# A three-block transformer kernel on one Trainium2 core: products of ones on an idle TensorE, and expert weights loaded expert by expert

## The reference

```
def moe(h, w_router, b_router, w_gate, b_gate, w_up, b_up, w_down, b_down):
    logits = jnp.dot(h, w_router) + b_router
    top_logit, top_idx = lax.top_k(logits, TOP_K)          # 4 of 32
    gates = jax.nn.softmax(top_logit, axis=-1)
    ...
    def expert_block(args):                                # rows of one expert
        xb, e = args
        g = jnp.minimum(xb @ w_gate[e] + b_gate[e], SWIGLU_LIMIT)
        u = jnp.clip(xb @ w_up[e] + b_up[e], -SWIGLU_LIMIT, SWIGLU_LIMIT)
        act = g * jax.nn.sigmoid(SWIGLU_ALPHA * g) * (u + 1)
        return act @ w_down[e] + b_down[e]
    ...
```

## Time and profile before

| | us |
|---|---|
| median of 3 runs | 2707.42 |
| lowest, highest | 2702.99, 2712.85 |
| profiled execution | 2703.1 |
| its span in the trace | 2701.4 |
| TensorE busy | 2512.8 (93%) |
| VectorE, ScalarE busy | 1056.0, 370.9 |
| read from memory | 726.30 MB |
| the half products of the experts, L1498: gate and up, down | 475.9, 240.4 |

### The profile page before, as it was taken

The page is one execution under the profiler, slowest core; times in us unless marked ns, Lnnn a source line. Parts: engine busy times, 40 slices in busy tenths (PEclk is TensorE's granted clock), DMA queues, the critical chain, the costliest instruction groups (busy, mean ns, idle before and its releaser), DMA issues. The chain is left out here.

```text
span 2701.4 us, 33603 instructions
## 1 busy us (share of the span) xinstructions
PE 2512.8 (93%) x12943; PEld 1534.0 (57%) x12944; DVE 1056.0 (39%) x2206; ACT 370.9 (14%) x747; POOL 43.0 (2%) x64
## 2 busy tenths in 40 slices
PE   6998999999999799997999989998999999988998
PEld 2543333333333233335878857867876887756786
DVE  1243122221121122224382258756996433244433
ACT  2122111111111111111122110011002000132001
POOL 0000000000000000000000000000100000000000
PEclk8998999999999899998989999999999999999999
DMA  8604999999997899998433368844997543141442
GB/s 333 264 9 165 427 429 429 428 429 428 428 429 335 341 428 429 428 410 313 167 125 133 148 222 331 289 162 155 379 380 273 195 166 109 69 156 36 144 165 100
DMA packets 188020, 728.26 MB, mean 270 GB/s; under 512 B 9758, under 2 KB 103292, under 8 KB 159156
## 3 DMA queue, kind: packets, MB, share of 16 engines
q1 hardware_dynamic: 168324, 651.29, 61.6%
q0 software_dynamic: 19632, 76.09, 7.1%
HBM read 726.30 MB, written 1.05 MB: 269 GB/s over the span
## 5 line engine op out<-in xcount | busy, mean ns | idle before, releaser
L1498 PE MATMUL bank<-experts_raw,experts_xs 128*64 128x512 f32 x2112 | 475.9, 600 | 15.9 <-DMA experts_raw<-in_w_up 13.6
L1498 PEld LDWEIGHTS bank<-experts_raw,experts_xs 128*64 128x64 f32 x2112 | 147.9, 138 | 334.5 <-issue 295.1
L2384 PE MATMUL bank<-big,ffn_actT 128*128 128x512 f32 x704 | 309.1, 592 | 0.0
L1498 PE MATMUL bank<-experts_raw,tiled_act_s 128*64 128x512 f32 x1056 | 240.4, 601 | 51.7 <-DMA experts_raw<-in_w_down 50.5
L1797 PE MATMUL bank<-hT,ring 128*128 128x256 f32 x1024 | 225.0, 383 | 4.1 <-DMA ring<-in_w_in 2.9
L1797 PEld LDWEIGHTS bank<-hT,ring 128*128 128x128 f32 x1024 | 196.7, 192 | 32.9 <-issue 5.8
L2384 PEld LDWEIGHTS bank<-big,ffn_actT 128*128 128x128 f32 x704 | 130.6, 190 | 148.3 <-issue 148.3
L1632 DVE COPY tiled_spread<-bank 128x256 f32<-128x256 f32 x33 | 14.0, 425 | 441.2 <-PE bank L1534 441.2
L1498 PEld LDWEIGHTS bank<-experts_raw,tiled_act_s 128*64 128x64 f32 x1056 | 71.1, 137 | 199.1 <-issue 122.4
L2259 PEld LDWEIGHTS bank<-hT,big 128*128 128x128 f32 x1408 | 164.4, 193 | 18.5 <-issue 18.5
L2259 PE MATMUL bank<-hT,big 128*128 128x128 f32 x1408 | 165.5, 276 | 0.3 <-DVE hT L454 0.3
(11 more groups left out here) (478 smaller groups left out, 2629.3 us busy)
## 6 DMA issues: line engine op xcount, KB each, us to landing
experts_raw<-in_w_gate SPq DMA_DIRECT2D x64, 2048.0 KB, 23.7
experts_raw<-in_w_up SPq DMA_DIRECT2D x64, 2048.0 KB, 25.1
experts_raw<-in_w_down SPq DMA_DIRECT2D x64, 2048.0 KB, 25.5
big<-in_ffn_w_gu SPq DMA_DIRECT2D x88, 1024.0 KB, 9.4
ring<-in_mod_w POOLq DMA_DIRECT2D x30, 2048.0 KB, 10.7
big<-in_ffn_w_down SPq DMA_DIRECT2D x44, 1024.0 KB, 5.0
ring<-in_w_in SPq DMA_DIRECT2D x16, 2048.0 KB, 8.6
mla_wm<-in_w_mod SPq DMA_DIRECT2D x24, 1024.0 KB, 6.7
```

Source lines behind the costliest of these rows:

```text
L1498: last = nc.tensor.matmul(bank[b][h * HALF:(h + 1) * HALF, :], stationary(kt), raw[p][:, k, h * C:(h + 1) * C], start=kt == 0, stop=kt == ...
L2384: last = nc.tensor.matmul(bank[b][:], actT[:, s, f, t * P:(t + 1) * P], wd[:, s, f, n * 512:(n + 1) * 512], start=start and f == 0, stop=s ...
```

## The change

It has two parts. A new helper, `warm(pe, b, n)`, lets TensorE compute n products of a 128 x 128 matrix of ones with itself into bank b; nobody reads them. It stands at 14 places in the program's text, at ends of stages, at the start of the norms that have their sum of squares already (`squared`), and at a few places inside the second block, the pooling mixer and the differential attention. In the numbers of one run it makes 9, 19, 5, 6 and 32 products in the first block, 6, 10 and 26 in the second, and 116 in the third: 229. The experts' stage gets another order: SP loads gate, up and down of one expert behind one another, and TensorE computes down of item e-1 right behind gate of item e.

```diff
+    def warm(self, pe, b, n):
+
+        for _ in range(n):
+            self.nc.tensor.matmul(self.bank[b][:, 0:P], self.ones[:], self.ones[:], start=True, stop=True)
...
@@ Norm.tensor
         for b in range(4):
             core.claim(pe, b)
+        if self.squared:
+            core.warm(pe, 0, 5)
         for t in range(TT):
...
@@ end of mla_norm, of mla_heads, of route
+                core.copied(pe, 7)
+                core.warm(pe, 7, 9)
...
+                core.warm(pe, 1, 19)
...
+            core.copied(pe, 5)
+            core.warm(pe, 5, 6)
...
@@ experts_tiled, SP
-            load(1, 0)
-            load(1, 1)
-            with sp.Fori(2, E) as e:
-                load(e, 0)
-                load(e, 1)
-                load(e - 1, 2)
-            load(E - 1, 2)
+
+            with sp.Fori(1, E) as e:
+                for m in range(3):
+                    load(e, m)
             core.first_w_in_2(sp)
...
@@ experts_tiled, TensorE
             with pe.Fori(1, items) as e:
-                gate_up(e)
+
+                expert = gate(e)
+                down(e - 1)
+                gather(e + 1)
                 turn(e + 1, g_rows, g_copied, G, g_turned)
+                up(e, expert)
                 spreading(e - 1, x_copied, e + 1)
-                down(e - 1)
                 after(pe, spread_ready, e)
                 turn(e + 1, x_rows, x_copied, X, x_turned)
                 turn(e + 1, u_rows, u_copied, U, u_turned)
                 scatter(e - 1)
...
             scatter(n - 1, True)
+            core.warm(pe, Y, 32)
...
@@ experts_tiled, ScalarE
             with act.Fori(1, items) as e:
-                take_gu(e)
+                take_g(e)
                 take_y(e - 1)
+                take_u(e)
                 take_x(e + 1)
...
@@ second
+                if h < 2:
+                    core.warm(pe, 0, (6, 10)[h])
                 core.claim(pe, b)
...
+            core.copied(pe, 7)
+            core.warm(pe, 7, 26)
...
@@ ffn, end; pool_mixer, start and end
+            core.copied(pe, 7)
+            core.warm(pe, 7, 9)
...
+            core.claim(pe, 4)
+            core.warm(pe, 4, 7)
             pe.wait_ge(*norm.normed.next(pe, TT))
...
+            core.warm(pe, 4, 9)
...
@@ diff_attention
+                core.claim(pe, b)
+                if h == H3 - 2:
+                    core.warm(pe, b, 6)
                 pe.wait_ge(*S["prob_ready"].next(pe, TT))
-                core.claim(pe, b)
...
+            core.copied(pe, 4)
+            core.warm(pe, 4, 10)
...
+                core.claim(pe, q)
+                if q == 0:
+                    core.warm(pe, q, 14)
                 pe.wait_ge(*S["o_ready"].next(pe))
-                core.claim(pe, q)
...
+            core.copied(pe, 7)
+            core.warm(pe, 7, 9)
```

More of the change, by code:

```diff
@@ L1500, in product, with gate @@
                     last.then_inc(used[p], 1)
-            def gate_up(e):
+            def gate(e):
                 after(pe, xs_ready, e)
@@ L1506, in gate_up, with up @@
                 product(expert, 0, G, lambda kt: tiles(xs)[:, kt % 4, kt // 4, :])
-                gather(e + 1)
+                return expert
+            def up(e, expert):
                 after(pe, u_taken, e)
@@ L1547, in scatter @@
                             op.then_inc(*core.filled[2 * t + h].up())
-            gate_up(0)
+            first = gate(0)
+            gather(1)
+            up(0, first)
             turn(1, g_rows, g_copied, G, g_turned)
@@ L1588, in take_y, with take_g, take_u @@
                 run(ys[:], bank[Y][:], ACT.Copy).then_inc(y_copied, 1)
-            def take_gu(e):
+            def take_g(e):
                 after(act, used[PARTS - 1], e + 1)
                 run(g_rows[:], bank[G][:], ACT.Copy).then_inc(g_copied, 1)
+            def take_u(e):
                 take_rows(e + 1)
@@ L1597, in take_gu @@
                 run(sig[:], gate[:], ACT.Sigmoid, scale=SWISH).then_inc(sig_ready, 1)
-            take_gu(0)
+            take_g(0)
+            take_u(0)
             take_x(1)
             with act.Fori(1, items) as e:
-                take_gu(e)
+                take_g(e)
                 take_y(e - 1)
+                take_u(e)
                 take_x(e + 1)
```

## The result

The changed kernel takes 2716.95 us (median of 6 runs, 2710.65 to 2722.73), the kernel before 2706.82 beside it. The ratio is 1.0041, 95% interval [1.0021, 1.0061]: 0.4% slower. 2719 was forecast, with +11.6 against the median of before; +10.1 came. The profiled execution of after is the shortest of the six (2710.65, span 2709.0).

The account below looks back on a forecast made before the run. Weight transfers were taken to bound the experts. To the profiled 2703.1 us it added 29.4 for the order and −18 for the ones, giving 2714.5; the median, 4.3 above, was forecast at 2719, range 2693 to 2744.

Parts of the forecast that it names:

- Bound: Experts: weight transfers at 428 GB/s set the pace, 29.36 us a round; TensorE's own round is shorter, 26.59.
- The steady round: Experts' loop: down's buffer comes free late, the queue runs dry 0.85 us a round, over 27 rounds +23.0.
- Start: Loop's first gate at clock 0.52 makes down's buffers late: +3.4 us.
- Expert with two items: Expert 20: the 15.07 us wait for down goes, gate, up and down of expert 21 wait instead: −4.0 us.
- Tail: Experts' end: last gate and up behind one more pair of transfers, +9.8 us; shorter work from that gate, −2.8.
- The ones: 229 products of ones keep TensorE's clock full: −21 and −1.5 gain, +4.5 cost, net −18 us.
- eleven stretches: Low-clock stretches at starts of stages, holding 51.66 us of TensorE work at half speed; full clock would save 25.8.
- The costs of the ones: Ends of stages: products of 0.28 us each running past the other engines' work, 4.5 us in total.
- Rival 1: Experts: the queue never runs dry, the 23.0 us vanish, total 2696; chance 0.22.
- rival 2: Ones do not hold or restore the clock where it matters, or run at low clock themselves; total 2740, chance 0.15.
- Rival 3: Clock falls in the experts' rounds, down's buffers come free later: +46 us, total 2765; chance 0.1.

Follow-up runs that it names:

- e3: Changed kernel with TensorE computing down of item e-1 ahead of gate of item e, ones kept; 2692.73 us, 0.9955 of the kernel before.
- e5: e3 plus VectorE's gate part ahead of the spread tokens' copy and turn u ahead of turn x; 2685.07 us, 0.9908 of the kernel before.
- e4: Changed kernel with the next item's gather ahead of down of item e-1 instead of behind it; 2768.14 us, 1.0225 of the kernel before.
- e2: Changed kernel without any products of ones, only the new experts' order; 2733.02 us, 1.0097 of the kernel before.
- e8: Changed kernel with 44 products of ones instead of 32 behind the experts' last scatter; 2715.83 us, 1.0038 of the kernel before.
- e1: Kernel before with its old experts' order, plus all 229 products of ones; 2696.79 us, 0.9959 of the kernel before.
- e7: The order of e5 without any products of ones; 2696.73 us, 0.9965 of the kernel before.
- e6: Kernel before plus only the ones ahead of the experts (9, 19, 5 and 6 products); 2707.05 us, 1.0016 of the kernel before.

## Why the prediction was right, step by step

- **Bound.** The transfers of weights set the pace, and TensorE's longer work in a round did not matter. Right: e3 to e5 move the time by moving when a buffer comes free.
- **The steady round (+23.0 forecast).** Mechanism right: down's buffer comes free 12.0 after gate's landing (12.2 forecast), the load lands 8.1 later (8.2), the queue runs dry. e3 takes the dry time away, e4 enlarges it by what was forecast. The size was off: 0.63 a round instead of 0.85, so 27 x 0.63 = 17 (e2: 0.77, 21; the landings give 0.6 and 0.7, and 0.45 in e8, so it differs between executions). Two small errors add up: the difference of a 12.2 and of an 8.2 from a 19.6 is so small that 0.2 in the parts is a quarter of the result.
- **Start (+3.4).** Too high. Gate's first product in the loop did run in part at the low clock (0.50 from 279.7 to 286.4, the product from 282.81), but the first load of down of the loop landed only 1.7 later than an unbroken stream would have it, and the kernel before lost nearly as much in its first loads: 4.1 by the landings, 4.8 in after.
- **Expert with two items (−4.0).** −2.5 by the windows (28.6 to 26.1), and each of the three parts within 1.1 of its forecast. Right that the 15-us wait would only change its place: now the loads of gate, up and down each wait.
- **Tail (+9.8 − 2.8).** The last gate begins at 1208.40 instead of 1184.65; from there 40.5 instead of 42.3, −1.8 where −2.8 was forecast. I had overlooked that TensorE before stood some 2 us behind the landing of that gate (at 1182.85 in the trace, product at 1184.65), which the new order doesn't (1208.36 and 1208.40).
- Together the stage's end is 22.0 later in the trace of after, 26.3 more in e2's; 29.4 was forecast.
- **The ones (−18 forecast).** This is the term that was furthest off: about −10 on the means of nine traces, −9.3 and −11.7 by e1 against before and e7 against e5. The step that failed is the share of the faster clock that reaches the end. First, I put all eleven stretches into the gain, and three of them (15.5 of the 51.66 us, some 6 of the forecast) lie ahead of the experts or at their start; e6 shows that nothing is won there. Second, I took off a fifth for what is not on the path. Added up over the traces, TensorE's work at the low clock behind the experts was 67.5 us in before and 23.0, 31.3, 23.4, 23.2 and 32.2 in after, e1, e3, e4 and e5; half of the difference is 18 to 22 us saved by TensorE, and "behind" got only 7.4 to 14.4 shorter. So a third to over a half of it was lost on the way, the time of the ones included; on which waits is not shown. A third, smaller part is that the clock did not hold over every barrier (in after at 1259 and 1614, worth 3.4 us at most), and in e1 again, 11 us at 0.53:

```profile
1245.00:1256.00 11.00, 8.57 (x28) 7.27 (x29) 1.51 (x4) 1.32 (x4) 1.63 (x2) 0.53 0.79 254
```

- The costs of the ones were smaller than the 4.5 forecast: 0.23 a product, not 0.28. The 32 end 1.0 ahead of ScalarE, and the 19 (234.04 + 4.40 = 238.4) end 0.9 ahead of it (239.3), so that neither barrier is later in after.
- The two errors have opposite signs (−7 and +8 against the traces), so that the sum came within 2 us. That part of the hit is luck; the sign is not: the order costs 22 to 27 and the ones bring 10.
- **Rivals.** Rival 1 (the queue never runs dry) fell with the 8.1 us and the 29.95; rival 2 (ones don't act on the clock) fell with e1 and with 1.00 at 2314, though it has a share in 1259 and 1614. Rival 3 shows once in after (at 556), and often only in e4.
- The Trainium skill's page "TensorE: Matmul & The Clock Gate" (Part 4: PE-mode transpose) says that transposes don't count for the full clock, and I drew from it that the ones would have to bring the clock alone. The runs differ. In e7, which has no ones, TensorE idled 10.23 us at the barrier behind the experts and then did nothing but these float32 transposes, at 421 ns each; 2.7 us later, still among the 16, they took 273 ns, as in e3 and e8 at the full clock. e6 has the same in 3.29 us instead of 3.65. The measurement decides: here the clock rose with no work but transposes since the wait. The two groups of the 16 in e7 (duration in ns: least, median, most):

```profile
L474 PE MATMUL bank<-ident,x x12: 421/421/445, 1232.9 to 1235.3; 128*128 128x128 f32 x12
L474 PE MATMUL bank<-ident,x x4: 273/273/344, 1235.5 to 1235.9; 128*128 128x128 f32 x4
```

- The estimate of a restart by the fit on the Trainium skill's page "DMA: Bandwidth & Descriptors" (Anatomy of one DMA), 6.8, was too low for these loads, which SP issues and not GpSimd; the trace has 8.1.

## What to carry to other kernels

Where transfers set the pace through one set of buffers, ask of each order of work when each buffer comes free, and compare that with the moment at which its next load must start to follow the one ahead without a gap; here 12 us against 11.5, and moving one product in front of another (e3) took a loss of 22 us away. Once the queue is full, the next bound (VectorE's chain to the activations) is close, and has to be moved as well before there is a gain (e5, and e7 without the ones). Work on an idle TensorE for the sake of its clock pays only where TensorE is what the end waits for (e6), roughly half of what it saved TensorE reached the end here, and products that run past the last work of the other engines put the barrier off by as much (e8: 1.7 us).

## What the runs showed that was not expected

The attention ahead of the experts is the same in all kernels, but in some executions its clock is low for 10 to 14 us at 146. The same window in the traces of before and of e1:

```profile
146.00:160.00 14.00, 13.04 (x40) 5.67 (x40) 6.66 (x20) 4.96 (x12) 0.00 (x0) 1.00 0.00 0
```

```profile
146.00:160.00 14.00, 14.00 (x17) 4.54 (x17) 4.19 (x12) 3.24 (x8) 0.00 (x0) 0.51 0.00 0
```

In these 14 us TensorE gets through 40 records of products at 1.00, and through 17 at 0.51, busy all the time. With it (clock 0.51 to 0.63 in this window) the first load of weights is at 247.6 to 251.7 (e1, e2, e3, e4, e5, e7, e8), without it (clock 1.00) at 241.4 to 242.7 (before, after, e6): 5 to 10 us, as much as the ones are worth. It comes in kernels with and without ones there. What decides it was not tried. It is why one span of one execution says little here: e1's profiled execution was as long as that of before (2701.2 against 2701.4), and its median 9.3 shorter.
